# One gather per layer and a straight run of 16 expert pairs in the expert stage of a two-layer decoder

## The reference, cut to what matters

```python
def hier_moe(h, w_rg, b_rg, w_re, b_re, w_gate, w_up, w_down):
    # h: 320 tokens x 1024
    # top-1 of 4 groups by h @ w_rg + b_rg; top-2 of the 8 experts of that group by h @ w_re + b_re
    # gate = p(group) * softmax(the two expert logits)
    # every token goes to its 2 of 32 experts:
    #   y += gate * (silu(h @ w_gate[e]) * (h @ w_up[e])) @ w_down[e]
```

## Time and profile before

| | |
|---|---|
| median of 3 runs | 2605.59 us (2603.42 to 2611.85) |
| the profiled execution | 2610.73 us, span of its trace 2608.9 us |
| PE busy | 2001.3 us, 77% of the span |
| DVE, ACT, POOL busy | 22%, 13%, 7% |
| mean granted TensorE clock | 0.832 of full speed |
| HBM traffic | 608.82 MB, 233 GB/s over the span |

### The profile page before, as it was taken

The page is one execution under the profiler, slowest core; times in us unless marked ns, Lnnn a source line. Parts: engine busy times, 40 slices in busy tenths (PEclk is TensorE's granted clock), DMA queues, the critical chain, the costliest instruction groups (busy, mean ns, idle before and its releaser), DMA issues.

```text
span 2608.9 us, 23329 instructions
## 1 busy us (share of the span) xinstructions
PE 2001.3 (77%) x9303; PEld 1029.0 (39%) x9303; DVE 563.6 (22%) x1052; ACT 330.0 (13%) x539; POOL 170.6 (7%) x203
## 2 busy tenths in 40 slices
PE   5698555657699999999778946455758999999983
PEld 2365342224433343343335634322443433334432
DVE  1222443333101111110203154433230110101002
ACT  1122101211010011000011130122100100110001
POOL 1000002330000000000000010142100000000000
PEclk9699556768599999999888965576857999999996
DMA  9521104893078888898791120188604888888870
GB/s 358 224 81 53 53 13 154 310 338 144 1 321 338 354 347 347 351 361 347 323 391 65 49 74 13 42 317 312 242 33 193 339 356 346 351 348 347 358 322 20
DMA packets 69533, 608.82 MB, mean 233 GB/s; under 512 B 9403, under 2 KB 9667, under 8 KB 36560
## 3 DMA queue, kind: packets, MB, share of 16 engines
q1 hardware_dynamic: 55296, 562.06, 54.0%
q0 software_dynamic: 14160, 45.70, 5.2%
HBM read 601.91 MB, written 5.81 MB: 233 GB/s over the span
## 4 chain that ended last, share of the span: by engine, by line
PE 70%; DVE 12%; DMA 7%; ACT 5%; issue 3%; POOLq 1%; POOL 1%; PEldq 0%; ACTq 0%; DVEq 0%; SPq 0%; PEld 0%
PE PS L961 26%; PE PS L931 9%; PE PS L557 8%; PE PS L942 6%; PE PS L479 4%; DVE big L1408 4%; PE PS L891 3%; DMA ring<-in_w_ada 3%; PE PS L837 2%; DMA ring<-in_sb_kv,idxu 2%; DVE mT L1408 2%; ACT big L1126 2%; PE PS L774 2%; ACT big L1122 1%; PE PS L512 1%
## 5 line engine op out<-in xcount | busy, mean ns | idle before, releaser
L961 PE MATMUL PS<-ring,big 128*64 128x512 f32 x3072 | 704.6, 612 | 65.2 <-POOLq L421 44.6
L961 PEld LDWEIGHTS PS<-ring,big 128*64 128x64 f32 x3072 | 221.1, 141 | 503.5 <-issue 493.1
L1126 ACT ACTIVATE big<-PS 128x512 f32<-128x512 f32 (+11 forms) x213 | 157.6, 750 | 1332.3 <-PE PS L479 419.8
L479 PE MATMUL PS<-cst,big 128*128 128x128 f32 (+5 forms) x557 | 113.1, 336 | 211.5 <-ACT big L1122 84.3
L931 PE MATMUL PS<-big 128*128 128x256 f32 (+1 forms) x768 | 239.2, 443 | 17.9 <-issue 13.5
L1408 DVE TENSOR_TENSOR big<-big,PS 128x320 f32<-128x320 f32 (+5 forms) x180 | 96.3, 542 | 649.3 <-PE PS L961 329.4
L557 PE MATMUL PS<-mT,ring 128*128 128x320 f32 x768 | 213.5, 439 | 1.9 <-PE PS L557 1.8
L479 PEld LDWEIGHTS PS<-cst,big 128*128 128x128 f32 (+5 forms) x557 | 76.4, 168 | 287.4 <-ACT big L1122 102.9
L931 PEld LDWEIGHTS PS<-big 128*128 128x128 f32 (+1 forms) x768 | 135.7, 204 | 119.3 <-issue 110.6
L557 PEld LDWEIGHTS PS<-mT,ring 128*128 128x128 f32 x768 | 146.7, 192 | 67.2 <-issue 8.2
L1408 DVE TENSOR_TENSOR big<-big 128x256 f32<-128x256 f32 (+8 forms) x144 | 60.6, 421 | 489.8 <-POOLq L421 439.1
(11 more groups left out here) (271 smaller groups left out, 1240.4 us busy)
## 6 DMA issues: line engine op xcount, KB each, us to landing
ring<-in_w_gate SPq DMA_DIRECT2D x64, 2048.0 KB, 8.8
ring<-in_w_up SPq DMA_DIRECT2D x64, 2048.0 KB
ring<-in_w_down SPq DMA_DIRECT2D x64, 2048.0 KB, 7.8
ring<-in_w_ada SPq DMA_DIRECT2D x24, 2048.0 KB, 10.8
ring<-in_sb_kv SPq DMA_DIRECT2D x128, 256.0 KB, 4.5
ring<-in_w_in SPq DMA_DIRECT2D x12, 2048.0 KB, 11.5
ring<-in_win_kT SPq DMA_DIRECT2D x8, 2048.0 KB
ring<-in_win_v SPq DMA_DIRECT2D x8, 2048.0 KB
```

Of the source, the lines that this page charges most:

```text
L479: return nc.tensor.transpose(out, in_, ident[0:in_.shape[0], 0:in_.shape[0]])
L961: i = mm(PS[SLOTS * x:SLOTS * x + SLOTS, out_bank + half, :], stationary(k, x), w, start=(k == 0), stop=(k == steps - 1))
L1126: return nc.scalar.activation(out, in_, ACT.Copy)
```

## The change

- **One gather per layer.** The experts' rows are sorted: `starts` holds where each expert's rows begin in a list of 640. DVE writes one-hot matrices of 640 columns once per layer, TensorE gathers all 640 columns at once (48 matmuls of 320 columns), and ACT and DVE copy them to `hsel` in turn. This now stands at the end of the output stage, ahead of its barrier.
- **Windows.** For each expert DVE loads its start into a register and copies 64 columns of `hsel` from that offset to `rows`, two pairs ahead.
- **Order.** The 16 pairs of a layer are written out one behind the other, without loop and without barriers between groups. Loads come as gate, up, down for each pair.
- **Release.** The counts of `ring_free` are moved. Those of a gate block stand behind the first step (two matmuls) of the up block that follows; those of a down block behind the first step of the next pair's gate block; those of an up block behind the slot sums.
- **Slot sums** are one matmul per d instead of two, 8 for each pair, as soon as the next pair's gate and up blocks are issued.
- The dense path gets barriers of its own, led by DVE. It is not taken here.

The core of the diff:

```diff
-GATE_AT, UP_AT, DOWN_AT = (0, 1, 4, 5), (2, 3, 6, 7), (8, 9, 10, 11)
+GATE_AT, UP_AT, DOWN_AT = (0, 1, 6, 7), (2, 3, 8, 9), (4, 5, 10, 11)
+OF_GATE, OF_UP, OF_DOWN = 0, 2, 4
+ROWS, PAIRS = 2 * T, NE // 2
...
-    out["iota"] = np.tile(np.arange(SLOTS), (128, 1))
+    out["iota"] = np.tile(np.arange(2 * T), (128, 1))
...
+            def gather():
                 pe.wait_ge(sem["picks"], 1)
+                pe.wait_ge(sem["rows_kept"], 3)
+                for k in range(KT8):
+                    for half in range(2):
+                        n = 2 * k + half
+                        if n >= 4:
+                            pe.wait_ge(sem["gathered_act" if half == 0 else "gathered_dve"], k - 1)
+                        for t, (t0, w) in enumerate(SPANS):
+                            i = mm(PS[:, n % 4, 0:T], moe.htok[0:w, t, k * 128:(k + 1) * 128],
+                                   moe.pick[0:w, t, half * T:(half + 1) * T], start=(t == 0), stop=(t == 2))
+                        i.then_inc(sem["gather_mm"], 1)
...
+                def arrived_pair(p, kind):
+                    for x in range(2):
+                        full(l, MOE0 + 6 * p + kind + x)
+
+                def release(p, kind):
+                    for x in range(2):
+                        pe.sem_inc(ring_free[(MOE0 + 6 * p + kind + x) % RING], 1)
+
+                def gate(p):
+                    rows = lambda k, x: M.rows[:, p % 4, k, x * SLOTS:(x + 1) * SLOTS]
+                    pe.wait_ge(sem["rows_windowed"], p + 1)
+                    if p:
+                        pe.wait_ge(sem["gate_act"], p)
+                    arrived_pair(p, OF_GATE)
+                    i = half_tile(p, OF_GATE, 0, 0, 0, 8, rows)
+                    if p:
+                        pe.wait_ge(sem["down_pair_mm"], p)
+                        release(p - 1, OF_DOWN)
+                    for k in range(1, 8):
+                        i = half_tile(p, OF_GATE, 0, 0, k, 8, rows)
+                    i.then_inc(sem["pair_mm"], 1)
+
+                def up(p):
...
+                    arrived_pair(p, OF_UP)
+                    half_tile(p, OF_UP, 1, 0, 0, 8, rows)
+                    pe.wait_ge(sem["pair_mm"], p + 1)
+                    release(p, OF_GATE)
+                    for k in range(1, 8):
+                        i = half_tile(p, OF_UP, 1, 0, k, 8, rows)
+                    i.then_inc(sem["up_pair_mm"], 1)
+
+                def slot_sums(p):
+                    pe.wait_ge(sem["slot_out_copied"], p + 1)
+                    pe.wait_ge(sem["spread_copied"], p + 1)
+                    for d in range(8):
+                        n = 8 * p + d
+                        if n >= 2:
+                            pe.wait_ge(sem["down_added"], n - 1)
+                        mm(PS[:, 6 + d % 2, 0:T], M.outs[:, p % 2, d * 128:(d + 1) * 128], M.spread[:, p % 2, :],
+                           start=True, stop=True).then_inc(sem["slot_sum_mm"], 1)
...
+                for p in range(PAIRS):
+                    gate(p)
+                    up(p)
+                    if p:
+                        slot_sums(p - 1)
+                    pe.wait_ge(sem["up_pair_mm"], p + 1)
+                    release(p, OF_UP)
+                    turn(p)
+                    turn_spread(p)
+                    down(p)
...
                 with pe.Else():
-                    gather(range(KT8))
-                    barrier(pe)
-                    group(l, 0, False, True)
-                    barrier(pe)
-                    with pe.Fori(1, NE // GE - 1) as it:
-                        group(l, it, True, True)
-                        barrier(pe)
-                    group(l, NE // GE - 1, True, False)
-                    barrier(pe)
-                    slot_sums(range(8))
+                    experts(l)
...
+            def window(p):
+
+                for x in range(2):
+                    e = 2 * p + x
+                    at = dve.value_load(starts[0:1, e:e + 1], min_val=0, max_val=ROWS)
+                    i = V.tensor_copy(moe.rows[:, p % 4, :, x * SLOTS:(x + 1) * SLOTS], moe.hsel[:, :, bass.ds(at, SLOTS)])
+                i.then_inc(sem["rows_windowed"], 1)
...
+                for p in range(PAIRS):
+                    if p + 1 < PAIRS:
+                        weigh_picks(p + 1)
+                    dve.wait_ge(sem["gate_act"], p + 1)
+                    dve.wait_ge(sem["up_pair_mm"], p + 1)
+                    tt(Mo.hid[:, p % 2, :], Mo.silu[p % 2], PS[:, 1, :], M_).then_inc(sem["hidden"], 1)
+                    if p:
+                        slot_sums(p - 1)
+                    if p + 2 < PAIRS:
+                        window(p + 2)
```

More of the change, by code:

```diff
@@ L250, in trunk @@
         crowded = sb("crowded", 1, I32)
+        starts = sb("starts", NE, I32)
         L3 = lambda off, a, b: v3(big, off, a, b)
@@ L935, in slot_sums @@
[L935 to L946, removed]
-                M = moe
[L953 to L996, removed]
-                if prev:
-                    slot_sums(range(4, 8))
-                pe.wait_ge(sem["weighted_picks"], 1)
-                for pair in range(2):
-                    for t, (t0, n) in enumerate(SPANS):
-                        i = tr(PS[:, 4 + pair, t0:t0 + n], M.wpick[0:n, t, pair * 128:(pair + 1) * 128])
-                i.then_inc(sem["spread_turned"], 1)
-                gate(1)
-                release(3, GATE_AT, 1)
-                if prev:
-                    pe.wait_ge(sem["down_added"], 8)
-                turn(0)
-                if more:
-                    gather((0, 1))
-                up(1)
-                release(4, UP_AT, 1)
-                if more:
-                    gather((2, 3))
-                pe.wait_ge(sem["spread_copied"], 1)
-                down(0)
-                release(5, DOWN_AT, 0)
-                turn(1)
-                if more:
-                    gather((4, 5, 6, 7))
-                down(1)
-                release(6, DOWN_AT, 1)
-                if not more:
-                    pe.wait_ge(sem["slot_out_copied"], 2)
@@ L1381, in _ @@
                             dense_expert(u)
[L1382 removed]
+                        dense_barrier(act)
                 with act.Else():
[L1384 to L1392 removed]
+                    experts()
                 barrier(act)
@@ L1855, in slot_sums @@
-            def slot_sums():
+                c(V.tensor_tensor_scan(Mo.start, K("ones1").to_broadcast([128, NE]), PS[:, 4, 96:128], 0.0, M_, A_))
+                c(tt(Mo.start, Mo.start, PS[:, 4, 96:128], S_))
+                c(V.tensor_copy(starts[:, :], Mo.start))
+                c(V.memset(Mo.pos, 0.0))
+                for n, t in ((128, slice(0, 2)), (64, slice(2, 3))):
+                    c(tt(Mo.pos[0:n, t, :], Mo.rank[0:n, t, :], spread(Mo.start[0:n], 1, t.stop - t.start), A_))
+                c(V.tensor_reduce(Mo.first, Mo.pos, AX.X, ALU.min))
@@ new lines, in stage_out @@
+                c(tt(Mo.pos, Mo.pos, Mo.selc, M_))
+                c(V.tensor_reduce(Mo.second, Mo.pos, AX.X, ALU.max))
+                for j, (t0, n) in enumerate(SPANS):
+                    ts(Mo.pick[0:n, j, :], K("iota")[0:n], Mo.first[0:n, j:j + 1], None, ALU.is_equal)
+                c(V.memset(Mo.hsel[:, :, ROWS:ROWS + SLOTS], 0.0))
+                for j, (t0, n) in enumerate(SPANS):
+                    i = stt(Mo.pick[0:n, j, :], K("iota")[0:n], Mo.second[0:n, j:j + 1], Mo.pick[0:n, j, :], ALU.is_equal, A_)
```

289 lines of the change are left out of this document (158 added, 131 removed).

## The result

The changed kernel takes 2769.11 us (median of 4 runs, 2748.07 to 2782.51) against 2608.72 us before on the same chips. The ratio is 1.061, 95% interval 1.058 to 1.065: slower by 6.1%. Forecast were 2736 us, slower by 5%. The profiled execution is one of the faster ones: 2756.94 us, span 2755.1.

A forecast was written before the change was run, and what follows sets the result against it. TensorE, busy 93% of the expert stage, was taken as the bound, with DMA close behind. 2610.7 us (profiled) + 127 for the stages + 3 for their start and constants = 2741, less 5.1 to the median: 2736 us, range 2625 to 2790.

The forecast's parts named there:

- The releases serialize the loads: Expert stage: gate and down releases wait for the next weights, so loads run singly; a pair goes from 35.6 to 40.45 us.
- A step of 13.4 us from arrival to arrival: Weight loads in a pair: 13.1 us for a lone load plus 0.3 for two matmuls, two such steps a pair.
- An up block of 9.25 us behind its wait: Up block on TensorE: after waiting some 4 to 6 us it runs at a lowered clock, 9.25 us against 7.09.
- TensorE stays fast: Rival: the up block takes 7.1 us, the gate load queues behind down, 108 us less, 2628 us; chance 13%.
- The release 4.7 us behind the up block: Slot sums behind the up block: eight sums on two banks delay the release of up's buffers by 4.7 us.
- The stage: Expert stage of each layer: ends 642.3 us after gate(0) starts, against 576.2 and 581.4 before, together 127 us lost.
- The start of the stage: From the last token copy to the first block: +1.2 us a layer, with +0.7 once for constants, together +3.
- the price of the gather: Gather at the stage's start: 96 records, clock raised after 5 us, 29.2 us against 25.30 before.
- The rival that it stays there: Rival: the gather stays at 1.2 GHz, 52.8 us long, 47 us more in all, 2783 us; chance 16%.
- The other terms: Start of the stage besides the gather: gather starts 5.5 us earlier; copy, barrier, load and windows behind it take 5.9 against 3.1.
- the largest term: The two expert stages: layers lose 66.1 and 60.9 us, together 127 us, of the forecast slowdown.

The follow-up runs named there:

- e1: Changed kernel with the gate, up and down releases put back right behind their blocks: 2674.65 us, ratio 1.027 to the kernel before.
- e2: Kernel before, with each release put behind the first two matmuls of the next block: 2716.3 us, ratio 1.043.
- e9: Changed kernel with only three dense 512-column matmuls (the burst) added ahead of the gather: 2737.03 us, ratio 1.049 to the kernel before.
- e3: Changed kernel with ten extra matmuls in TensorE's wait ahead of each up block: 2704.99 us, ratio 1.039 to the kernel before.
- e6: Changed kernel with releases right behind blocks and slot sums split, four behind gate and four behind down: 2576.57 us, ratio 0.990 to the kernel before.
- e7: e6 with three extra dense 512-column matmuls ahead of the gather: 2543.18 us, ratio 0.977 to the kernel before.
- e10: Kernel before with three dense 512-column matmuls ahead of the first gather of each layer: 2594.05 us, ratio 0.995.

## Why the prediction was right, step by step

- **The releases serialize the loads: right.** The wait ahead of each gate and up block, the loads issued 0.1 us behind a block's start, and the DMA engines idle in between are all in the trace. e1 takes the late releases away and nothing else, and e2 adds them to the kernel before and nothing else.
- **A step of 13.4 us from arrival to arrival: right.** From gate to up it is 12.7 us on average in the first layer (838.07 to 851.05 is 13.0) and 13.9 in the second. From the release of the up buffers to the next gate block, 864.46 to 878.30, it is 13.8 us, where I had 13.1.
- **An up block of 9.25 us behind its wait: a little high.** In the first layer it is 8.2 us on average. In every second pair from the fifth on it is 7.09, as at 890.92 behind a wait of 3.83 us. That is just under the shortest wait of the earlier trace rows, but the length of the wait alone does not decide: at 811.04 a block behind 3.06 us took 8.49. The period of a pair with such a fast block is 38.4 us and of the others 40, and the rival "TensorE stays fast" thus came true in part. In the second layer the up blocks take 9.3 us on average, as forecast, and the period is 40.7.
- **The release 4.7 us behind the up block: right.** The block ends at 859.84, the release in the chain of waits stands at 864.46: 4.6 us.
- **The stage: 642 us forecast, 626.5 and 646.0 measured.** That is a loss of 115 us where I had 127. The stage moved 320 GB/s at a DMA share of 0.81, where I had 311 at 0.73.
- **The start of the stage: mis-sized, +3 us forecast, +37 measured.** The failed step was the price of the gather, "9 x 0.55 + 87 x 0.278 = 29.2 us". The gathers took 39.3 and 53.6 us. First, the clock was raised only after 15 us in the first layer and 43 in the second. I had taken 5 us from matmuls with the same 320 columns, while the nearest row by kind was the gather itself, 25.3 us at 1.2 GHz. The rival that it stays there had got 16%. Second, a record at 2.4 GHz takes 0.334 us here (32.07/96), not the 0.278 of the old gathers (3.34/12). The other terms held: 1.2 us from the last transpose to the gather, and 6.3 us from its end to the first block where I had 5.9.
- **The clock of the gather as the spread of the runs.** Since the time until the clock rises differs from 15 to 43 us between two gathers of one execution, it may explain part of the 34 us between the fastest and the slowest run. That is argued, not tested: with the burst (e9) the four runs lie within 13 us, which fits, but those of e3 lie within 11 without one.

The total was within 1.2% because the largest term was right, and in part by luck, since the errors of the stages and of their start have opposite signs. The errors are -12 us for the stages, +34 for their start, -6 elsewhere, and +17 because this profiled execution stands 12 us below its median where that of before stood 5 above.

## What to carry to other kernels

In a ring the place where a buffer is given back counts as much as its size: if the release stands behind a wait for the next load, the loads run one by one, and each costs its full latency. For each buffer, write down what lies between the end of its use and the next use of the same buffer; it must be at least the time of a lone load, and other work belongs where this is too short. Removing work from an engine that is 93% busy gives little when the next transfers are set off late: even with releases and sums well placed (e6) it was 1%. Where a stage begins at the low clock and its matmuls leave it there for long, try a few matmuls of 512 columns in front: they took 0.5% off the kernel before and 1.2 points off the changed one.

## What the runs showed of the hardware

- Two loads of 2 MB, 4.19 MB, issued to idle DMA engines take 11.9 to 14.1 us from the second issue to landing, by the chain of waits of the changed kernel, nearly all of them under 13.6. In the first layer of e6, where a load is issued while another runs, it is 13.7 to 16.2 us. The best stage (e7) moved 376 GB/s.
- The same 96 matmul records of 320 columns took 32.07 us with the clock up from the start, and 37.5 to 53.6 us when they began at 1.2 GHz, where the clock rose after 15 and after 43 us of back-to-back matmuls in one execution. Dense numbers in place of the one-hot matrices did not change that (44.0 and 45.8 us). Six records of 512 columns in front did, in both layers of e7 and of e9, and the 48 records of 256 columns of the kernel before went from 25.3 to 13.7 us behind them (e10).
- Extra matmuls in TensorE's wait ahead of up (e3) brought its blocks back from 8.2 and 9.3 us to 7.1 to 7.2 on average, and made the two stages 38 us shorter.
